# Dispatch to the experts as two single-pass products on token rows split into a high and a low part

## What is computed

```python
def moe_swiglu(h, router_w, wg, wu, wd):
    logits = (h @ router_w).astype(jnp.float32)
    top_v, top_i = lax.top_k(logits, TOP_K)
    gates = jax.nn.softmax(top_v, axis=-1)
    comb = jnp.sum(jax.nn.one_hot(top_i, N_EXPERTS, dtype=jnp.float32) * gates[..., None], axis=-2)
    out = jnp.zeros_like(h)
    for e in range(N_EXPERTS):
        out = out + comb[..., e:e + 1].astype(h.dtype) * swiglu(h, wg[e], wu[e], wd[e])
    return out
```

## Time and profile before

| | |
|---|---|
| median of 3 runs | 1951.87 us (1950.73 to 1960.22) |
| the profiled execution, its own time | 1950.87 us |
| its span | 1949.2 us |
| PE busy in the span | 1778.6 us, 91% |
| weight loads on PE (PEld), busy | 1515.9 us, 78% |
| DVE busy | 1359.4 us, 70% |
| ACT busy | 1039.4 us, 53% |
| POOL busy | 47.7 us, 2% |
| the dispatch's matmuls, L2029 | 44.3 us busy, 384 records, 2% of the chain |
| the loop of experts | from 930.88 us to the end of the span |

### The profile page before, as it was taken

How to read it: one execution, slowest core, us unless ns; L and a number is a source line. 1 busy time by engine, 2 the same in 40 slices (tenths; PEclk the granted TensorE clock), 3 DMA queues, 4 the chain that set the end, 5 groups by cost and what they waited for, 6 DMA issues and landing times.

```text
span 1949.2 us, 25409 instructions
## 1 busy us (share of the span) xinstructions
PE 1778.6 (91%) x9791; PEld 1515.9 (78%) x9791; DVE 1359.4 (70%) x1563; ACT 1039.4 (53%) x964; POOL 47.7 (2%) x100
## 2 busy tenths in 40 slices
PE   4976889999998677788999999999999999999997
PEld 4945779998996666547788888888888888888886
DVE  3565234454675666455788988889888898898886
ACT  3452133343554122003777777777777677777674
POOL 2012000000001000101000000000000000000000
PEclk9975679998897888659999999999999999999999
DMA  6343124455243000322798998999989989899894
GB/s 205 133 169 112 44 87 173 138 187 179 87 173 115 1 1 1 98 86 99 254 378 320 364 373 315 361 340 354 378 301 374 357 328 369 320 367 374 310 368 149
DMA packets 199083, 445.49 MB, mean 229 GB/s; under 512 B 9457, under 2 KB 20883, under 8 KB 198959
## 3 DMA queue, kind: packets, MB, share of 16 engines
q1 hardware_dynamic: 182206, 423.75, 59.8%
q0 software_dynamic: 3872, 12.85, 2.3%
q10 hardware_dynamic: 12924, 7.77, 1.3%
HBM read 437.28 MB, written 7.29 MB: 228 GB/s over the span
## 4 chain that ended last, share of the span: by engine, by line
PE 81%; DVE 9%; ACT 4%; DMA 1%; issue 1%; PEld 1%; ACTq 1%; POOLq 0%; PEldq 0%; POOL 0%; DVEq 0%
PE bank L2079 16%; PE bank L2058 11%; PE bank L2059 10%; PE bank L2063 10%; PE bank L769 5%; PE bank L773 5%; PE bank L778 5%; PE bank L2029 2%; DVE weight_lo L470 2%; DVE work L1353 1%; ACT weight_hi L467 1%; PE bank L1899 1%; PE bank L2039 1%; PE bank L714 1%; PE bank L1957 1%
## 5 line engine op out<-in xcount | busy, mean ns | idle before, releaser
L470 DVE TENSOR_TENSOR weight_lo<-weight_ring,weight_hi 128x2048 fp32r<-128x2048 f32 (+1 forms) x358 | 809.7, 2272 | 300.6 <-ACT weight_hi L467 300.6
L467 ACT ACTIVATE weight_hi<-weight_ring 128x2048 fp32r<-128x2048 f32 (+1 forms) x358 | 680.2, 1904 | 334.5 <-PE bank L778 142.3
L2058 PE MATMUL bank<-weight_hi,h_lo 128*128 128x512 f32 x896 | 355.2, 396 | 4.2 <-DVE h_lo L1566 4.2
L2059 PE MATMUL bank<-weight_hi,h_hi 128*128 128x512 f32 x896 | 349.9, 391 | 0.0
L2063 PE MATMUL bank<-weight_lo,h_hi 128*128 128x512 f32 x896 | 239.8, 389 | 0.0
L769 PE MATMUL bank<-h_hi,weight_hi 128*128 128x264 f32 x1072 | 189.8, 293 | 18.4 <-ACT h_hi L743 10.4
L2058 PEld LDWEIGHTS bank<-weight_hi,h_lo 128*128 128x128 f32 x896 | 168.9, 188 | 38.8 <-DVE h_lo L1566 4.5
L2063 PEld LDWEIGHTS bank<-weight_lo,h_hi 128*128 128x128 f32 x896 | 168.2, 188 | 35.1
L2059 PEld LDWEIGHTS bank<-weight_hi,h_hi 128*128 128x128 f32 x896 | 169.0, 189 | 33.5
L773 PE MATMUL bank<-h_hi,weight_lo 128*128 128x264 f32 x1072 | 185.7, 288 | 1.9 <-DVE weight_lo L470 1.9
L778 PE MATMUL bank<-h_lo,weight_hi 128*128 128x264 f32 x1072 | 184.7, 287 | 0.0
(11 more groups left out here) (438 smaller groups left out, 1725.5 us busy)
## 6 DMA issues: line engine op xcount, KB each, us to landing
weight_ring<-in_moe_wg SPq DMA_DIRECT2D x104, 1024.0 KB, 6.3
weight_ring<-in_moe_wu SPq DMA_DIRECT2D x96, 1024.0 KB, 7.2
weight_ring<-in_moe_wd SPq DMA_DIRECT2D x88, 1024.0 KB, 6.2
work<-in_moe_wd SPq DMA_DIRECT2D x24, 1024.0 KB, 6.5
weight_ring<-in_w_in_o SPq DMA_DIRECT2D x8, 2048.0 KB, 8.5
work<-in_moe_wu SPq DMA_DIRECT2D x16, 1024.0 KB, 5.9
weight_ring<-in_w_in_e SPq DMA_DIRECT2D x5, 2048.0 KB, 13.4
weight_ring<-in_ffn_wg SPq DMA_DIRECT2D x5, 2048.0 KB, 7.8
```

Source lines behind the costliest of these rows:

```text
L467: return SC.activation(whi[:, p % SPLIT, 0:size], src, ACT.Copy).then_inc(sig("hi_done"), 1)
L470: V.tensor_tensor(wlo[:, p % SPLIT, 0:size], src, whi[:, p % SPLIT, 0:size].bitcast(F32), ALU.subtract)\
L2058: PE.matmul(out, hte_l[:, j, :], hi[:, jj, :], start=j == 0, stop=False)
L2059: PE.matmul(out, hte_h[:, j, :], hi[:, jj, :], start=False, stop=False)
```

## The change

`h_tok` is replaced by two buffers, `hk_hi` and `hk_lo`, which hold the high and the low part of each token row in fp32r. `sel` becomes fp32r too; its zeros and ones need no low part. All three are views of one new tile, `token_split`, that takes the last 6528 columns of the place where `work` lies. `dispatch` makes two fp32r matmuls where it made one fp32 matmul. ACT's eviction now writes `hk_hi`. DVE makes `hk_lo` out of the same PSUM tile with six new instructions, after `select(0)` and ahead of the work on the gates. PE waits for those (`htok_lo`) where it had waited for ACT (`htok`), before it overwrites the PSUM tiles with the rows of `xT` and before the first dispatch. POOL zeroes the whole of `token_split`, once the sample states have been written out; DVE's two memsets are gone, and ACT and DVE wait for POOL (`tokens_zero`).

```diff
-        h_tok = cut(QKV0, NTT, D)
-        raw_last = cut(QKV0 + NTT * D, PIECE)
+        hk_hi, hk_lo = (moe_r[:, k * NTT * D:(k + 1) * NTT * D].rearrange("p (t d) -> p t d", t=NTT) for k in range(2))
+        sel = moe_r[:, 2 * NTT * D:].rearrange("p (t c) -> p t c", t=NTT)
+        raw_last = cut(QKV0, PIECE)
...
+            for k in range(4):
+                gp.wait_ge(*at(f"state{k}_written", 32))
+            GP.memset(moe_r[:].bitcast(F32), 0.0).then_inc(sig("tokens_zero"), 1)
             for m in range(1, KD):
                 gp.wait_ge(*at("norm3_sq", m + 1))
...
             act_e.wait_ge(*at("norm3_inv", 1))
+            act_e.wait_ge(*at("tokens_zero", 1))
...
-                    SC.activation(h_tok[0:n, i, k * CHUNK_COLS:(k + 1) * CHUNK_COLS], bank[k * 4 + i][0:n, :], ACT.Copy,
+                    SC.activation(hk_hi[0:n, i, k * CHUNK_COLS:(k + 1) * CHUNK_COLS], bank[k * 4 + i][0:n, :], ACT.Copy,
                                   scale=rstd[0:n, i:i + 1]).then_inc(sig("htok"), 1)
...
-            V.memset(h_tok[:, TT, :], 0.0)
-            V.memset(sel[:, TT, :], 0.0)
...
+            dve.wait_ge(*at("tokens_zero", 1))
             select(0)
+            for k in range(YC):
+                for i, (t0, n) in enumerate(TOK):
+                    cols = slice(k * CHUNK_COLS, (k + 1) * CHUNK_COLS)
+                    dve.wait_ge(*at("htok", k * NTT + i + 1))
+                    V.scalar_tensor_tensor(hk_lo[0:n, i, cols], bank[k * 4 + i][0:n, :], rstd[0:n, i:i + 1], hk_hi[0:n, i, cols].bitcast(F32),
+                                           ALU.mult, ALU.subtract).then_inc(sig("htok_lo"), 1)
...
-            pe.wait_ge(*at("htok", NTT))
+            pe.wait_ge(*at("htok_lo", NTT))
             token_rows(xT, 0, "xtok_psum")
-            pe.wait_ge(*at("htok", NTT * YC))
+            pe.wait_ge(*at("htok_lo", NTT * YC))
...
-                        last = PE.matmul(bank[(7, 3)[r]][:, jj * CAP:(jj + 1) * CAP], h_tok[:, i, j * P:(j + 1) * P],
-                                         sel[:, i, :], start=i == 0, stop=i == NTT - 1)
+                        out = bank[(7, 3)[r]][:, jj * CAP:(jj + 1) * CAP]
+                        PE.matmul(out, hk_hi[:, i, j * P:(j + 1) * P], sel[:, i, :], start=i == 0, stop=False)
+                        last = PE.matmul(out, hk_lo[:, i, j * P:(j + 1) * P], sel[:, i, :], start=False, stop=i == NTT - 1)
```

More of the change, by code:

```diff
@@ L156, in program @@
         W = 17696
-        work = sb("work", [P, W])
+        MOE_R = (TT + 1) * (2 * D + P)
+        with nc.sbuf_tensor("work", [P, W], F32) as work:
+            pass
+        sb("work_rest", [P, W - MOE_R])
+        moe_r = sb("token_split", [P, MOE_R], F32R)
         bank = [ctx.enter_context(nc.psum_tensor(f"bank{i}", [P, CHUNK_COLS], F32)) for i in range(8)]
@@ L405, in program @@
         assert NTT * D + 4 * CHUNK_COLS <= INV0
-        h_tok = cut(QKV0, NTT, D)
-        raw_last = cut(QKV0 + NTT * D, PIECE)
-        mo = [QKV0 + NTT * D + PIECE]
+        hk_hi, hk_lo = (moe_r[:, k * NTT * D:(k + 1) * NTT * D].rearrange("p (t d) -> p t d", t=NTT) for k in range(2))
+        sel = moe_r[:, 2 * NTT * D:].rearrange("p (t c) -> p t c", t=NTT)
+        raw_last = cut(QKV0, PIECE)
+        mo = [QKV0 + PIECE]
+        assert W - MOE_R >= QKV0 + PIECE
         def more_of(*dims):
@@ L412, in more_of @@
             mo[0] += math.prod(dims)
-            assert mo[0] <= W
+            assert mo[0] <= W - MOE_R
             return v
-        sel = more_of(NTT, CAP)
         iota = more_of(P)
@@ L2116, in pe_expert @@
                         for i in range(NTT):
-                            last = PE.transpose(bank[4][:, i * P:(i + 1) * P], sel[:, i, :], ident[:])
+                            last = PE.transpose(bank[4][:, i * P:(i + 1) * P], sel[:, i, :].bitcast(F32), ident[:])
                         last.then_inc(sig("moe_w"), 1)
```

## The result

The changed kernel takes 1963.97 us (median of 5 runs, 1962.2 to 1967.9) against 1951.87 of the kernel before on the same chip: 12.1 us more, a ratio of 1.0059 with a 95% interval of 1.0042 to 1.0076. The forecast was 1956.0 us, 4.1 over that median, with a range from 1936 to 1963: the sign of the difference was right, but it is three times as large, and the time lies 1.0 us over the range. It is also over the 9.8 us that the prediction set as its bound between same and slower; slower had a chance of 0.16. The profiled execution of after took 1965.39 us with a span of 1963.8.

What follows compares the result with a forecast made beforehand. The prediction took PE to bound the loop of experts, and loads to bound the dispatch. 1950.9 (profiled execution) + 0 (dispatch) + 4.3 (DVE) + 0.8 (clock) = 1956.0 us, range 1936 to 1963.

Steps and rivals of the forecast that it cites:

- The dispatch is load-bound, 0 gained: All eight dispatches: pairs of load and matmul stay 0.110 us apart, a dispatch stays at 5.3 us, 0 gained.
- Rival A: Dispatch: the load shrinks too, 0.065 us a pair, 17.3 us less for eight, 1938.7 us; chance 0.14.
- Rival B: Dispatch: narrow fp32r products take 0.22 us each, 42 us more for eight, 1998 us; chance 0.12.
- Six DVE instructions, 4.26 us on the path: Ahead of the loop, behind `select(0)`: six new DVE instructions delay the first dispatch by 4.26 us, once.
- Memsets on POOL and DVE, 0: Ahead of the loop: POOL's 6.1 us memset is covered by its own wait, DVE's dropped memsets gain nothing; 0.
- The clock in that wait, 0.8 us: Ahead of the first dispatch: PE stands still 3.8 us, the granted clock falls, 0.8 us lost.
- The sign named for it: Ahead of the loop: the first expert product starts at about 935 to 936 instead of 930.88.
- the two conditions under which the prediction called itself wrong: fp32r loads shorter than its trace rows make them, or the loop of experts waiting for anything but PE.
- Its upper end, 4.9 us: First dispatch: clock loss if half rate lasted over the whole dispatch, 48 x 0.1 = 4.9 us.
- Rival C: Head of the loop: clock costs 4.9 us, not 0.8, plus 1 us beside POOL's memset; 1961 us, no separate chance.

Runs made afterwards that it cites:

- high parts alone: The changed kernel with only the 24 high-part products of the 48 in each dispatch, low parts computed but not used: 1945.42 us (one run).
- the kernel with work for PE: The changed kernel plus eight unused fp32 products on PE while DVE makes the low parts: 1959.34 us, ratio 1.0014 to the kernel before.
- the kernel without low parts: The changed kernel without DVE's six instructions, PE waiting for ACT as before, 48 products kept: 1955.46 us, ratio 1.0003 to the kernel before.

## Why the prediction was right and wrong

- *The dispatch is load-bound, 0 gained:* right, and shown from three sides. Pairs stay 0.11 us apart with 64 columns and take 0.12 with 256; products with loads of 8 columns follow 0.03 us apart; and the time goes with the number of pairs (high parts alone). The rule for loads in the Trainium skill, "TensorE: Matmul & The Clock Gate", section "LDWEIGHTS (loading the stationary operand)", gives an estimate of 107 ns for 128 columns; the trace agrees, with 112 ns a pair (5.39 / 48). Rival A (a load that shrinks) falls with the same rows.
- *Rival B (narrow fp32r products are dear):* doesn't hold at full clock; 0.112 us a pair is under its 0.122 (0.125 if the forecast's 4.1 us over the median is taken off the bound, and not 5.1). The 0.213 of the first dispatch is close to the 0.22 that it named, but it is the clock's: with PE kept busy in the wait the same dispatch takes 5.41 us.
- *Six DVE instructions, 4.26 us on the path:* right. They took 4.02 and put 3.94 on the path; in the kernel with work for PE, 3.86.
- *Memsets on POOL and DVE, 0:* right, by the rows above and by the kernel without low parts.
- *The clock in that wait, 0.8 us:* this is the step that failed. It measured 6.49 us. The wait itself was foretold to a tenth of a microsecond, and that the clock falls in it was foretold too. The size was carried over from another place, 3.1 us at half rate (1.55 us lost) behind a wait of 4.16 us, and then halved. But there PE goes on with products of 512 columns, and here with a dispatch during which the clock stays at half until the dispatch and the transposes are through. The first dispatch in fp32, and the one with 256 columns, show that what PE does behind the wait decides: 6.83 us at half rate in both, instead of 17.07. The two other kernels that begin with narrow fp32r products behind the same wait agree with after: 17.07 us with 64 columns, 20.48 with the high parts alone. The trace of before could have warned that the size doesn't carry over: by its clock records half rate lasts between 3.4 and 75.1 us there, and the stretch at the first product is of the shortest. The sign named for it, a first product at 935 to 936, failed plainly, with 944.00; but neither of the two conditions under which the prediction called itself wrong came true, for the clock was in neither.
- *Its upper end, 4.9 us (48 x 0.1 is 4.8):* the right size for the dispatch (4.85 measured), but it stood for "half rate over the whole dispatch" and left out the transposes on both sides of it, 0.42 and 1.22 us. Rival C had that end, and was called only the edge of the forecast. With 6.49 in place of 0.8 the sum gives 1961.7 us, inside the range; the median is 2.3 above that. The head's 10.43 us lie within the interval of the measured difference, 8.2 to 14.8 us (1.0042 to 1.0076), so no other cause is needed, and a small one isn't excluded.

## What to carry to other kernels

Before a product is split into cheaper ones, read whether its load or its matmul sets the pace. The narrow product here was bound by its load: it gained nothing from cheaper matmuls, and gained from putting the wide side on the moving operand. A new wait on PE can cost its own length and then the half rate behind it. That second part is to be sized by the work that follows the wait: behind the same wait of 3.67 us it lasted 6.83 or 17.07 us. Here both costs vanished when the other engine's new work was put into an idle time that it already had.

## What was not expected of the hardware

A stream of fp32r pairs with 128 moving columns kept the full clock once it had it (seven dispatches of 5.39 us at 1.00), and stayed at half for 10.28 us when it began there, with PE busy all the time. With 64 columns it lost the clock after 3.4 us in the loop without any wait; with 256 columns, or with fp32 products of 128, it got it back within the first half of the dispatch. Why the clock came back in the one and not in the other, the runs don't show.
